# Routing taken in four batches with its row table built by one-hot products, and the hidden rows of an expert block transposed ahead of the next block's rows

## The reference

```python
g_prob = softmax(t @ w_rg + b_rg);  g_p, g_idx = top_k(g_prob, 1)       # one of 4 groups
e_logits = (t @ w_re + b_re) of the chosen group                       # 8 experts in it
e_p, e_idx = top_k(softmax(e_logits), 2);  e_p = e_p / sum(e_p)
weights, expert = g_p * e_p, g_idx * 8 + e_idx
order = argsort(expert, stable);  counts = bincount(expert, 32)
padded = ceil(counts / 128) * 128                                      # MOE_BLOCK = 128
dest = start of the expert in the padded list + rank within the expert
row_tok[dest], row_w[dest] = token, weight      # unused rows: token N (a row of zeros), weight 0
block_e = owner of each block of 128 rows
for each block: xb = t_pad[rows]; y = (silu(xb @ w_gate[e]) * (xb @ w_up[e])) @ w_down[e]
y[row_tok] += y_rows * row_w
```

## Time and profile before

| what | value |
|---|---|
| median of 3 runs | 3861.3 us (3853.53 to 3864.49) |
| the profiled execution | 3858.22 us, of which the span from first to last instruction is 3856.4 us |
| busy in the span | PE 91%, DVE 44%, ACT 27%, POOL 26% |
| logit loop | about 2818 to 3123 us |
| routing | about 3124 to 3207 us |
| expert loop | about 3207 us to the end |

### The profile page before, as it was taken

How to read it: one execution, slowest core, us unless ns; L and a number is a source line. 1 busy time by engine, 2 the same in 40 slices (tenths; PEclk the granted TensorE clock), 3 DMA queues, 4 the chain that set the end, 5 groups by cost and what they waited for, 6 DMA issues and landing times. The chain is left out here.

```text
span 3856.4 us, 32998 instructions
## 1 busy us (share of the span) xinstructions
PE 3514.5 (91%) x11379; PEld 1831.0 (47%) x11379; DVE 1680.2 (44%) x3966; ACT 1036.2 (27%) x2537; POOL 1015.3 (26%) x1396
## 2 busy tenths in 40 slices
PE   4999999999999889989999988999899935999997
PEld 3744455555446444434444445555555522444443
DVE  4665633343453663336665556534533340212221
ACT  3121222211100540012244446433322211222221
POOL 0377767300000870000000006645600012121211
PEclk7999999999999999999999989999989967999999
DMA  3134445433263012222310000001022205999997
GB/s 133 60 123 151 158 141 163 146 108 123 78 207 113 14 66 82 82 93 72 116 50 22 11 11 1 1 1 66 11 74 84 97 23 220 328 325 328 327 330 235
DMA packets 116746, 460.10 MB, mean 119 GB/s; under 512 B 14643, under 2 KB 42291, under 8 KB 104540
## 3 DMA queue, kind: packets, MB, share of 16 engines
q1 hardware_dynamic: 91644, 370.32, 27.0%
q0 software_dynamic: 19456, 67.15, 6.2%
q10 hardware_dynamic: 5472, 20.45, 1.4%
HBM read 340.35 MB, written 117.52 MB: 119 GB/s over the span
## 5 line engine op out<-in xcount | busy, mean ns | idle before, releaser
L143 PE MATMUL pst<-arena 128*128 128x512 f32 (+5 forms) x6938 | 2759.7, 556 | 88.2 <-DVE arena L159 34.1
L143 PEld LDWEIGHTS pst<-arena 128*128 128x128 f32 x6938 | 1301.9, 198 | 1424.3 <-issue 1266.5
L165 POOL TENSOR_TENSOR arena<-arena 128x4 f32<-128x4 f32 (+7 forms) x784 | 409.6, 522 | 464.2 <-DVE arena L2025 403.8
L148 PE MATMUL pst<-arena 128*128 128x128 f32 (+1 forms) x2147 | 322.4, 289 | 195.2 <-DVE arena L247 52.5
L165 DVE TENSOR_TENSOR arena<-arena 128x1 f32<-128x1 f32 (+8 forms) x1233 | 446.2, 362 | 94.5 <-ACT arena L2255 20.2
L148 PEld LDWEIGHTS pst<-arena 128*128 128x128 f32 (+1 forms) x2147 | 257.1, 147 | 353.6 <-issue 143.2
L1287 POOL TENSOR_SCALAR arena<-arena 128x384 f32<-128x384 f32 (+1 forms) x128 | 151.7, 1203 | 563.7 <-DVE arena L1279 563.7
L154 ACT ACTIVATE arena<-pst,arena 128x128 f32<-128x128 f32 (+1 forms) x630 | 244.0, 482 | 144.8 <-PE pst L148 142.3
L2202 POOL TENSOR_SCALAR arena<-arena 128x512 f32<-128x512 f32 (+3 forms) x160 | 218.8, 1386 | 172.2 <-DVE arena L165 158.6
L174 ACT ACTIVATE arena<-arena 128x1024 f32<-128x1024 f32 x48 | 50.7, 1057 | 645.5 <-DVE arena L1523 373.4
L168 DVE TENSOR_SCALAR arena<-arena 128x1 f32<-128x1 f32 (+10 forms) x569 | 139.6, 245 | 190.6 <-DMA arena<-in_bc 78.8
(11 more groups left out here) (193 smaller groups left out, 2019.2 us busy)
## 6 DMA issues: line engine op xcount, KB each, us to landing
arena<-in_w_exp SPq DMA_DIRECT2D x48, 3072.0 KB, 12.0
arena<-in_w_ada SPq DMA_DIRECT2D x48, 512.0 KB, 4.7
rotd<-arena POOLq DMA_DIRECT2D x32, 512.0 KB, 4.0
arena<-rotd SPq DMA_DIRECT2D x32, 512.0 KB, 4.5
arena<-sgd SPq DMA_DIRECT2D x16, 1024.0 KB, 7.6
arena<-pwd SPq DMA_DIRECT2D x32, 416.0 KB, 5.6
pwd<-arena SPq DMA_DIRECT2D x16, 576.0 KB, 5.9
h2d<-arena SPq DMA_DIRECT2D x17, 512.0 KB, 2.9
```

Of the source, the lines that this page charges most:

```text
L143: x = t.do.matmul(o, l, r, start=(i == 0), stop=(i == len(pairs) - 1))
L148: x = t.do.transpose(o, i, ident[0:i.shape[0], 0:i.shape[0]])
L165: own(v, s).tensor_tensor(o, a, b, op).then_inc(*inc(s, *event))
```

## The change

1. The routing is cut into batches of four tiles. `ve_rt_pick` (the picks, `OH`, `cum`), `ve_rt_weights` and `ve_rt_rows` (the ranks) of batches 0 to 2 stand inside the logit loop of DVE, at the ends of steps 5, 9, 13 and 7, 11, 15 and 8, 12, 16; PE's rank products stand at the ends of its steps 7, 11, 15, in columns 128 to 255 of bank 7; ACT's exponentials ahead of steps 6, 10, 14. The four passes over the groups become one product with a one-hot row of the group and one sum. Batch 3 follows the last logits.
2. PE's product for the counts comes ahead of the last ranks. The block owners `bE` are made right after the starts, and the positions later.
3. There is no table in HBM. A choice's row within its block and its block number are made apart. `OHr` is one-hot in the row (128 columns), `Rv` one-hot in the block (64 columns) times token and times weight. PE adds up 32 products `OHr`(transposed) x `Rv` in bank 4, which gives ids and weights of all blocks. The scatters, the store of the padding and the read back are gone.
4. SP's weight loads wait for `bE` and for the last output stores instead of `rt_done`. The second buffer moves to kilobyte 24, so that no buffer lies over the new tables.
5. In the expert loop PE's two transposes of the hidden rows of b-1 become `te_moe_hidden`, ahead of `turn(b+1)`.

The core of the diff:

```diff
+        def te_rt(t):
+            t.wait_ge(*at("rt_ve", "cum", 3))
+            t.wait_ge(*at("o2_ve", "lg", NT - 1))
+            t.do.matmul(bank(6)[:, 0:32], ones, cum[:, 16, :], start=True, stop=True).then_inc(*inc("rt_pe", "count"))
+            te_rt_ranks(t, 3)
+            t.wait_ge(*at("rt_ve", "owner"))
+            trs(t, [(bank(6)[0:1, 0:128], bcol[:, 1:2])]).then_inc(*inc("rt_pe", "bE"))
+            t.wait_ge(*at("o2_ac", "xnT", NT - 1, 1))
+            for n in range(32):
+                k, i = n // 16, n % 16
+                t.wait_ge(*at("rt_ve", "Rv", k))
+                x = t.do.matmul(bank(4)[:, 0:128], OHr[:, k, i, :], Rv[:, n, :, :].rearrange("p a b -> p (a b)"),
+                                start=(n == 0), stop=(n == 31))
+            x.then_inc(*inc("rt_pe", "idT"))
...
-            for k in range(2):
-                for i in range(NT):
-                    p.do.indirect_dma_start(
-                        out=rtf, out_offset=bass.IndirectOffsetOnAxis(ap=posu[:, k, i:i + 1], axis=0),
-                        in_=tw[:, k, i, :], in_offset=None).then_inc(*dma("st_sct", "sct", k, i))
...
+                if i in (5, 9, 13, 17):
+                    ve_rt_pick(v, i // 4 - 1)
+                if i in (7, 11, 15):
+                    ve_rt_weights(v, i // 4 - 1)
+                if i in (8, 12, 16):
+                    ve_rt_rows(v, i // 4 - 2)
...
+            for k in range(2):
+                kk = slice(16 * k, 16 * k + 16)
+                tt(v, q, big[:, kk, :], bc(blk[:, k, :], 2, [128, 16, 64]), bc(io128[:, 0:64], 1, [128, 16, 64]),
+                   ALU.is_equal)
+                tt(v, q, Rv[:, kk, 0, :], big[:, kk, :], bc(tv[:, k, :], 2, [128, 16, 64]), MUL)
+                tt(v, q, Rv[:, kk, 1, :], big[:, kk, :], bc(tw[:, k, :], 2, [128, 16, 64]), MUL, "Rv", k)
...
-        WX = [reg(64, 6144), reg(128, 6144), reg(0, 6144)]
+        WX = [reg(64, 6144), reg(24, 6144), reg(0, 6144)]
...
         def sp_moe_load(s, b):
-            rt_done(s)
+            for i in range(2):
+                s.wait_ge(*at(f"st_out{i}", "x3", NT - 2 + i))
...
                 if b < hi:
                     te_moe_up(t, b)
+                if b > lo:
+                    te_moe_hidden(t, b - 1)
                 if b + 1 < hi:
                     te_moe_turn(t, b + 1)
```

More of the change, by code:

```diff
@@ L2427, in te_o2_sums @@
         def te_o2_sums(t, b):
+            t.wait_ge(*at("rt_ve", "row", b - 3))
             for i in range(4 * b, 4 * b + 4):
@@ L2545, in build @@
         gp = reg(99.75, 16)
-        tw = reg(100, 2, 16, 2)
-        eid = reg(100.25, 2, 16)
-        io32 = reg(100.5, 32)
+        tw = reg(100, 2, 16)
+        tv = reg(100.25, 2, 16)
+        io128 = reg(100.5, 128)
         OH = reg(101, 2, 16, 32)
@@ L2551, in build @@
         cum = reg(107, 17, 32)
-        pre = reg(109.5, 16, 32)
+        eid = reg(109.25, 2, 16)
+        rank, blk = reg(109.5, 2, 16), reg(109.75, 2, 16)
+        row, tokS = reg(110, 2, 16), reg(110.25, 16)
+        ge = reg(110.5, 4, 4, 8)
+        gh = reg(111, 4, 4)
         cnt = reg(111.5, 32)
@@ L2597, in te_rt @@
[L2597 to L2615, removed]
+        def te_rt_ranks(t, b):
+            t.wait_ge(*at("rt_ve", "cum", b))
+            t.wait_ge(*at("const_po", "tri"))
+            t.wait_ge(*at("o2_ve", "sums", min(3, b + 2)))
+            t.wait_ge(*at("rt_ve", "row", b - 1))
+            t.do.matmul(bank(7)[:, 128:256], tri, both[:, batch(b), :].rearrange("p a b -> p (a b)"), start=True,
+                        stop=False)
+            t.do.matmul(bank(7)[:, 128:256], ones, cum[:, batch(b), :].rearrange("p a b -> p (a b)"), start=False,
+                        stop=True).then_inc(*inc("rt_pe", "ranks", b))
@@ L2619, in ve_rt @@
             o2_done(v)
[L2620 to L2626, removed]
-                own(v, q).max_index(gi[:, i, :].bitcast(U32), gm[:, i, :], g8[:, i, :]).then_inc(*inc(q))
-            own(v, q).tensor_copy(gid, gi[:, :, 0].bitcast(U32)).then_inc(*inc(q))
@@ L2638, in ve_rt @@
-            for i in range(NT):
-                own(v, q).max(em_[:, i, :], e8_[:, i, :]).then_inc(*inc(q))
-            for i in range(NT):
-                own(v, q).max_index(ei[:, i, :].bitcast(U32), em_[:, i, :], e8_[:, i, :]).then_inc(*inc(q))
-            tt(v, q, t16, em_[:, :, 1], em_[:, :, 0], SUB, "gap")
-            v.wait_ge(*at("rt_ac", "gap"))
-            ts(v, q, u16, t16, 1.0, None, ADD, BYP)
-            own(v, q).reciprocal(u16, u16).then_inc(*inc(q))
-            tt(v, q, tw[:, 0, :, 1], u16, gp, MUL)
@@ L2654, in ve_rt @@
-            for i in range(NT):
-                tt(v, q, cum[:, i + 1, :], cum[:, i, :], both[:, i, :], ADD, *(["cum"] if i == NT - 1 else []))
-            v.wait_ge(*at("rt_pe", "ranks"))
-            own(v, q).tensor_copy(cnt, bank(7)[:, 0:32]).then_inc(*inc(q))
+            v.wait_ge(*at("rt_pe", "count"))
+            own(v, q).tensor_copy(cnt, bank(6)[:, 0:32]).then_inc(*inc(q))
             ts(v, q, pen, cnt, 63.25, 1.0 / 128, ADD, MUL)
```

147 lines of the change are left out of this document (98 added, 49 removed).

## The result

The changed kernel takes 3803.9 us (median of 4 runs, 3797.4 to 3813.9) against 3861.4 us: a ratio of 0.9855, with a 95% interval of 0.9839 to 0.9871. That is 57 us less where 55 were forecast (3806), and inside the range of 3794 to 3817.

What follows compares the result with a forecast made beforehand. Serial routing and scatters before the first expert block, then a loop near full on DMA (96%) and PE. Block 0's turn moves from 3217.57 to 3162.5, 55.1 us off the 3861.3 median: 3806 us, range 3794 to 3817.

Steps and rivals of the forecast that it cites:

- The last logits: End of the logit loop: moves from 3123.4 to 3124.4 us in trace time, with batches 0 to 2 routed inside.
- the 1.0 us for the rank products: PE in the logit loop: rank products added in three steps, 0.45 us each, taken as 1.0 us for all.
- From logits to ids: Batch 3's path after the logits: pick 7.0 us, count 0.8, owners 2.4, turn and cast 0.6; first load 1.05 later.
- The products: PE's 32 table products, 64 instructions: 7.2 us at full clock, 14.5 at half; end taken as 3157.
- The landing: First gather, issued at 3158.0 about when the three weight loads end: 4.5 us, where it was 10.4.
- landing in under 5 us: Sign that the forecast is right: the first gather, issued near 3158, lands in under 5 us.
- This is not worth 71.6 us: First weight loads start 71.6 us earlier, but only clear the way for the gather, since load 3 still needs `down(0)`.
- Rival 3: Early weight loads count in full, DMA alone setting the end: 71.6 us saved, 3790 us; chance 3%.
- The reorder: Expert loop, hidden rows turned before the next rows: price 0, since DVE's copy stands behind two operations of block b.
- rival 4: Routing not covered in the logit loop: up to 36 us, 3842 us, or 3824 with half of them; chance 7%.
- rival 2: Expert loop: the reorder pays too, removing the 0.69 us wait once per two blocks, 15 us, 3791 us; chance 6%.
- rival 5: Expert loop: slower, as turning hidden rows first delays the next rows, needing 3.1 us in every block; chance 1%.

Runs made afterwards that it cites:

- the one without batches: Changed kernel with all picks, ranks and weights of batches 0 to 2 moved out of the logit loop, behind the last logits: 3845.6 us, 0.9964 of before.
- the doubled products: Changed kernel with PE doing the 32 table products twice, the second pass restarting the sum: 3818.6 us, 0.9895 of before.
- four buffers: Changed kernel with a fourth weight buffer, its first load waiting for the ids, DVE's order unchanged: 3788.4 us, 0.9811 of before.
- half weights: Changed kernel with each weight load bringing only half its columns, output not the reference's: 3777.3 us, 0.9790 of before.
- late loads: Changed kernel with SP's weight loads waiting again for the ids and all stores: 3809.6 us, 0.9857 of before.
- the copy first: Changed kernel with DVE copying the hidden rows of block b-1 ahead of gating block b: 3791.9 us, 0.9818 of before.
- the held load: Changed kernel with a fourth weight buffer, DVE's hidden-row copy first, fourth load waiting for block 0's turn: 3768.4 us, 0.9759 of before.

## Why the prediction was right

*The last logits.* Forecast 3124.4, measured 3122.7. The absolute time can't test the 1.0 us for the rank products: in the twelve profiles of kernels with the same code up to there (all but the one without batches) PE's last logits end between 3108.6 and 3132.9, a spread that comes from the phases before. From DVE's first evacuation in the loop on, the twelve lie 1.1 to 2.6 us above the kernel before and up to 1.2 above the one without batches, which fits 1.0.

*From logits to ids*, each from its own start: pick and sums 7.0 forecast, 7.25 measured; count 0.8 and 0.73; counts to owners in SBUF 3.0 and 3.1; first load 1.05 and 1.07 behind them. From the logits to the start of the products 22.7 and 22.9. Its parts hold one by one as well: rows and weights of batch 3 took 5.3 us for 5.3, the start table 2.8 for 2.8. Small DVE operations at 0.2 us each, counted one by one, were an exact measure.

*The products*, 9.9 forecast (3147.1 to 3157), 8.8 measured. The clock rose 3 us after they began, for 4 in the forecast, and the doubled products took 7.24 us for 64 instructions at full clock, which is the 0.113 us of the row used. Half clock throughout (14.5) came true in no run; the longest took 10.4 (four buffers), with the clock rising after some 6 us. So a microsecond or two of this term was luck of the run.

*The landing*, 4.5 forecast, 5.6 measured from issue to turn, so the sign "landing in under 5 us" was not met. The forecast let the gather go out as the loads end. It went out at 3155.5, and the loads were still at work until about 3158. Where they had ended, in the runs with half weights, without batches and with doubled products, it took 4.3 to 4.4, so the term was right for its condition, and the condition was missed. One term was a microsecond short, the products a microsecond long; turn(0) came at 3161.1 for 3162.5, and relative to the logits 38.4 for 38.1. That these two cancel is only in part luck: faster products bring the gather nearer to the loads.

*The loads.* "This is not worth 71.6 us" held: they started 73.1 us earlier, E did not change, and late loads cost 6.4 to 6.7 us. Rival 3 is out. The Trainium skill (DMA: Bandwidth & Descriptors, Specifications) gives about 358 GB/s as the limit of HBM for one core, as half of a stack's 716. The trace goes above it again: 413 GB/s over 22 us, with three loads and the first gather. The kernel runs on one core only, so no run here shows what two would get.

*The reorder* at price 0 held, and for the reason given: DVE's own order. Putting DVE's copy first removed the wait, and putting PE's order back did not bring a longer one. The experiments show more than the argument did, that PE's order becomes worth something once DVE's is turned as well.

*The logit loop* hid all three batches; rival 4 is out (the gap behind a pick takes up what it is late, and the loop is at most about 1 us longer than without the picks).

*What was weak.* "DMA at 96%, which leaves little to gain" stood against rival 2. It was the wrong reason beside the right one: with the copy first E gained 16 to 22 us, and with a fourth buffer 21 to 26. The share itself was not far off. It left 4%, which of some 640 us is 26, and between 3300 and 3700 us it rose to 0.99 and 1.01 in these two kernels. Small as a share, this is not small against a gain of 57. In the changed kernel a load took 11.9 us of a block's 12.8, and each waited for a `down` before it could start. Two smaller slips changed nothing: PE did not idle at half clock through the whole routing of before (it did rank products until 3155.6, at a mean clock of 0.89 near their end, as the prediction itself says further down), and by its own numbers rival 5 needs 3.2 us for each block (2.0 + 55/47), not 3.1.

## What to carry to other kernels

A busy share of 0.96 of DMA does not say that nothing is left to gain: 4% of a long loop can be half of what a large change brings. Look at how many loads are in flight and what each waits for: here each load waited for the buffer of a block that was just being finished, and a fourth buffer removed the same waits as halving the bytes did.

Before moving an instruction forward on one engine, look at what stands ahead of its consumer on the other. Two orders that were worth nothing measurable alone were worth some 16 us together.

A long serial stretch between two dense loops is best cut where it can be spread into the idle gaps of the loop ahead: 37 of the 57 us came from that. Leaving out the 32 scatters, 1.3 us apart, gave, with the early loads and once the new work was paid for, 19 us in that stretch (14 by the total, with an uncertainty of 5).

## What was not expected of the hardware

Three plain loads of 3 MB ran at 413 GB/s together, at a share of 0.97, but the loop with its gathers and accumulating scatters moved 322 to 345 GB/s between 3300 and 3700 us (most with four buffers and the held load), at busy shares of 0.95 to 1.01. With half the weight bytes the share was 0.74 at 213 GB/s. So busy share and bytes do not go together one to one.

A single load beside the first gather more than doubled its landing: 13.1 to 13.3 us from issue to turn with a fourth load, 12.4 with three, 5.6 behind three that were nearly done, 4.3 to 4.4 behind three that were done.
